# Hybrid decoder trunk: the low parts of the tokens on Pool, and the norm before the experts in two halves

## What is computed

```python
for layer in range(DEPTH):                       # 2
    mix = even_mixer(...) if layer % 2 == 0 else odd_mixer(...)
    x = layer_norm(DN_ALPHA * x + mix, ln1_g[layer], ln1_b[layer])
    ff = moe_ffn(x, router_w[layer], ...)        # top 8 of 64 experts, 4 of 8 groups, and a shared expert
    x = layer_norm(DN_ALPHA * x + ff, ln2_g[layer], ln2_b[layer])
```

## Time and profile before

| | |
|---|---|
| median of 3 runs | 1240.02 us (1238.58 to 1240.29) |
| the profiled execution | 1239.59 us |
| its span | 1237.9 us, 18023 instructions |
| PE busy | 1181.5 us (95%) |
| DVE busy | 401.8 us (32%) |
| ACT busy | 297.8 us (24%) |
| Pool busy | 29.1 us (2%) |
| chain that ended last, by engine | PE 79%, DMA 15%, DVE 4%, ACT 1% |
| data moved by DMA | 445.19 MB, mean 360 GB/s |

### The profile page before, as it was taken

One profiled execution on the slowest core, in us unless ns is written; L12 is line 12 of the kernel. 1 busy time (PEld: TensorE's weight loads), 2 busy tenths in 40 slices (PEclk: granted clock), 3 DMA queues, 4 the chain that ended last, 5 costly groups with the idle time before them and its releaser, 6 DMA issues.

```text
span 1237.9 us, 18023 instructions
## 1 busy us (share of the span) xinstructions
PE 1181.5 (95%) x7212; PEld 539.4 (44%) x7212; DVE 401.8 (32%) x900; ACT 297.8 (24%) x652; POOL 29.1 (2%) x104
## 2 busy tenths in 40 slices
PE   8998999999999999999879999999999999999985
PEld 5776754434333433434236555343443434343421
DVE  3767274212121211212243656322221212121223
ACT  3354332212121211222121353121221112121212
POOL 1005000000000000000000000000000000000000
PEclk9999999999999999999999999999999999999998
DMA  9408059999999999999993657899999999999993
GB/s 368 176 1 315 37 211 424 415 416 426 429 428 429 427 429 427 430 428 428 424 390 139 272 204 279 351 415 411 427 429 428 429 428 429 428 429 429 427 425 146
DMA packets 44177, 445.19 MB, mean 360 GB/s; under 512 B 8016, under 2 KB 9168, under 8 KB 18016
## 3 DMA queue, kind: packets, MB, share of 16 engines
q1 hardware_dynamic: 43824, 444.25, 85.9%
q10 hardware_dynamic: 304, 0.26, 0.1%
HBM read 443.45 MB, written 1.05 MB: 359 GB/s over the span
## 4 chain that ended last, share of the span: by engine, by line
PE 79%; DMA 15%; DVE 4%; ACT 1%; issue 1%; DVEq 0%; SPq 0%
PE psum L429 29%; PE psum L510 16%; DMA w_down_ring<-in_moe_down 10%; PE psum L443 5%; PE psum L517 5%; PE psum L2522 4%; PE psum L2371 4%; PE psum L1392 3%; DMA w_up_ring<-in_moe_up 3%; PE psum L679 2%; PE psum L492 1%; PE psum L1875 1%; PE psum L713 1%; PE psum L2528 1%; PE psum L1703 1%
## 5 line engine op out<-in xcount | busy, mean ns | idle before, releaser
L429 PE MATMUL psum<-w_up_ring,moe_x_selected 128*64 128x512 f32 x2048 | 461.1, 597 | 12.3 <-DMA w_up_ring<-in_moe_up 11.8
L429 PEld LDWEIGHTS psum<-w_up_ring,moe_x_selected 128*64 128x64 f32 x2048 | 139.6, 137 | 296.7 <-issue 277.8
L1219 DVE TENSOR_TENSOR moe_out_low<-psum,moe_out_high 128x512 fp32r<-128x512 f32 x128 | 88.1, 691 | 356.7 <-ACT moe_out_high L968 356.7
L510 PE MATMUL psum<-w_down_ring,moe_hT 128*32 128x512 f32 x1536 | 178.6, 596 | 6.1 <-DMA w_down_ring<-in_moe_down 5.2
L968 ACT CAST moe_out_high<-psum 128x512 fp32r<-128x512 f32 x128 | 74.6, 586 | 262.0 <-PE psum L510 188.1
L1209 DVE SCALAR_TENSOR_TENSOR moe_h<-moe_silu,moe_slot_gate,psum 128x256 f32<-128x256 f32 x64 | 30.7, 480 | 285.6 <-ACT moe_silu L947 285.3
L510 PEld LDWEIGHTS psum<-w_down_ring,moe_hT 128*32 128x32 f32 x1536 | 44.2, 109 | 112.5 <-issue 100.4
L947 ACT ACTIVATE moe_silu<-psum 128x256 f32<-128x256 f32 x64 | 24.5, 383 | 208.1 <-PE psum L429 208.1
L951 ACT COPY moe_hT<-psum 128x256 f32<-128x256 f32 x64 | 23.8, 372 | 199.1 <-PE psum L492 199.1
L517 PE MATMUL psum<-moe_out_high,moe_matchT 128*128 128x512 f32 x128 | 57.0, 445 | 1.5 <-DVE moe_out_low L1219 1.5
L2371 PE MATMUL psum<-w_up_ring,mixed_transposed 128*128 128x512 f32 x128 | 56.6, 594 | 0.7 <-ACT mixed_transposed L2146 0.7
(11 more groups left out here) (537 smaller groups left out, 1012.4 us busy)
## 6 DMA issues: line engine op xcount, KB each, us to landing
w_up_ring<-in_moe_up SPq DMA_DIRECT2D x128, 2048.0 KB, 19.7
w_down_ring<-in_moe_down SPq DMA_DIRECT2D x48, 2048.0 KB, 20.6
norm_and_tokens<-in_moe_down SPq DMA_DIRECT2D x12, 2048.0 KB, 16.8
w_up_ring<-in_ev_columns SPq DMA_DIRECT2D x4, 2048.0 KB, 16.7
w_up_ring<-in_od_w_in SPq DMA_DIRECT2D x4, 2048.0 KB, 18.0
w_up_ring<-in_ev_out SPq DMA_DIRECT2D x2, 2048.0 KB, 8.1
moe_first_down<-in_moe_down SPq DMA_DIRECT2D x2, 2048.0 KB, 10.0
norm_and_tokens<-in_moe_down SPq DMA_DIRECT2D x4, 1024.0 KB, 11.6
```

The source lines that it names most:

```text
L429: last = nc.tensor.matmul(k.psum[e * SLOTS:(e + 1) * SLOTS, bank, :], xsel[:, kk, own:own + SLOTS], up_view(par, e, kk), start=kk == 0, st ...
L510: last = nc.tensor.matmul(k.psum[e * CAPACITY:(e + 1) * CAPACITY, unit_bank[n], :], hT[:, e // 2, own:own + CAPACITY], places[e][:, j, :], ...
L1219: nc.vector.tensor_tensor(low[:, own], k.psum[:, unit_bank[n], :], high[:, own], ALU.subtract).then_inc(s.low, 1)
```

## The change

- `low_part` moves from DVE to Pool, for both tiles. Pool waits there for the normed tile and for the high part. DVE waits for `parts` once, before it adds high and low again at the end.
- The last step of the first norm is two instructions of 512 columns, each with a signal on `normed1`, which now counts to two for each tile. PE waits for one half before four of the eight transposes; ACT's high part, Pool's low part and SP's load wait for both.

```diff
--- before.py
+++ after.py
@@ -561,7 +561,7 @@
             sp.wait_ge(s.mixed, 1 + e)
             load_up_half(sp, k, d, layer, 1, 1, e - 2, gu[1][e - 2])
         sp.dma_start(k.mixT[:].rearrange("p k t -> p (k t)"), d.shared_down[layer]).then_inc(s.shared_wd, 16)
-        sp.wait_ge(s.normed1, NT)
+        sp.wait_ge(s.normed1, 2 * NT)
         load_down_part(sp, norm_down, d, layer, 1, 1, 0, x.dn_norm)
         sp.wait_ge(s.xT_psum, 2 * NT)
         sp.wait_ge(s.parts, NT)
@@ -659,8 +659,8 @@
                 output_product(nc, k, t, half, chunks, begin=False).then_inc(s.mixed, 1)
 
         def turn_x(t):
-            pe.wait_ge(s.normed1, t + 1)
             for b in range(2):
+                pe.wait_ge(s.normed1, 2 * t + b + 1)
                 for c in range(4):
                     last = nc.tensor.transpose(k.psum[:, 4 + b, c * P:(c + 1) * P], k.x[:, t, (4 * b + c) * P:(4 * b + c + 1) * P],
                                                k.ident[:])
@@ -908,7 +908,7 @@
                                k.psum[:, 4 + b, :].rearrange("p (c n) -> p c n", c=4)).then_inc(s.xT, 1)
 
         def high_part(t):
-            act.wait_ge(s.normed1, t + 1)
+            act.wait_ge(s.normed1, 2 * t + 2)
             nc.scalar.copy(x_high[:, t].rearrange("p k c -> p (k c)"), k.x[:, t, :]).then_inc(s.x_high, 1)
 
         def scores(t):
@@ -1053,6 +1053,15 @@
     def gpsimd(pool):
         mixer.gpsimd(pool)
 
+        def low_part(t):
+            pool.wait_ge(s.normed1, 2 * t + 2)
+            pool.wait_ge(s.x_high, t + 1)
+            nc.gpsimd.tensor_tensor(x_low[:, t].rearrange("p k c -> p (k c)"), k.x[:, t, :],
+                                    x_high[:, t].rearrange("p k c -> p (k c)"), ALU.subtract).then_inc(s.parts, 1)
+
+        for t in range(NT):
+            low_part(t)
+
         def gates_of(q):
 
             nc.gpsimd.tensor_copy(quad_gates[:], gate_parts[:, :, bass.ds(8 * q, 8), :]).then_inc(s.quad_gates, 1)
@@ -1075,25 +1084,20 @@
         step(nc.vector.memset(w.ln_eps[:], LN_EPS))
         nc.vector.memset(w1.ln_eps[:], LN_EPS).then_inc(s.eps, 1)
 
-        def low_part(t):
-            dve.wait_ge(s.x_high, t + 1)
-            dve.wait_ge(s.normed1, t + 1)
-            nc.vector.tensor_tensor(x_low[:, t].rearrange("p k c -> p (k c)"), k.x[:, t, :],
-                                    x_high[:, t].rearrange("p k c -> p (k c)"), ALU.subtract).then_inc(s.parts, 1)
-
         for t in range(NT):
             for half in range(2):
                 dve.wait_ge(s.mixed, 2 * t + half + 1)
                 step(residual(nc, k, w1, t, half))
                 step(statistics(nc, dve, step, w1, t, half))
-                if (t, half) == (1, 0):
-                    low_part(0)
             nc.vector.bn_aggr(w1.meanvar[:, t, :], w1.bn[:, t, :, :]).then_inc(s.variance1, 1)
             dve.wait_ge(s.variance1, t + 1)
             step(gain_centred(nc, k, w1, t, w1.meanvar[:, t, 0:1], ALU.subtract))
             dve.wait_ge(s.root1, t + 1)
             step(nc.vector.reciprocal(w1.rstd[:, t:t + 1], w1.root[:, t:t + 1]))
-            scale_shifted(nc, k, w1, t).then_inc(s.normed1, 1)
+            for half in range(2):
+                cols = slice(half * BANK, (half + 1) * BANK)
+                nc.vector.scalar_tensor_tensor(k.x[:, t, cols], w1.resid[:, t, cols], w1.rstd[:, t:t + 1], k.ln[:, 1, cols], ALU.mult,
+                                               ALU.add).then_inc(s.normed1, 1)
 
         def group_heads(t):
             dve.wait_ge(s.scores, t + 1)
@@ -1134,7 +1138,6 @@
         dve.wait_ge(x.router, 32)
         group_heads(0)
         select(0)
-        low_part(1)
         place_of(0)
         first_match(0, s.early_match)
         group_heads(1)
@@ -1267,6 +1270,7 @@
         with dve.Fori(1, QUADS - 1) as q:
             quad(q)
         dve.wait_ge(s.down, 8 * (QUADS - 2) + 6)
+        dve.wait_ge(s.parts, NT)
         for t in range(NT):
             step(nc.vector.tensor_tensor(k.x[:, t, :], x_high[:, t].rearrange("p k c -> p (k c)"),
                                          x_low[:, t].rearrange("p k c -> p (k c)"), ALU.add))
```

## The result

The changed kernel takes **1243.28 us** (median of 20 runs, 1239.71 to 1244.94), the kernel before on the same chip 1240.82 us (20 runs, 1238.48 to 1242.70). The ratio is 1.0018, with an interval of 1.0012 to 1.0024: **2.2 us slower, 1.5 to 3.0**. The forecast was +0.8. What happened is rival two with both races lost: Pool was first at the selection too.

The account below looks back on a forecast made before the run. Weight loads pace the expert loops' ends, but DVE's path to the first match matrix before them carries through one for one. Pool holding the match adds +0.48 and +0.34, +0.8 on 1240.02: 1240.8 us, range 1238.3 to 1242.4.

Parts of the forecast that it names:

- rival two: Selection of tile 0: Pool starts first and holds DVE; +0.98 and +0.85 us, 1241.3 with one race lost, 1241.9 both; chance 0.14.
- who is first at the selection: Selection of tile 0: DVE's L1123 starts before Pool's subtract, by 0.05 us in layer 0 and 0.13 in layer 1.
- Two of 512 columns: First norm on DVE: two halves take about 1.3 us where one instruction takes 1.28; DVE loses 0.02 at most.
- The low part of tile 0: Moved to Pool: no gain in layer 0, where DVE makes it while waiting for PE; about 0.20 us in layer 1.
- Pool starts some 0.06 later: Subtract of tile 1, layer 0: Pool starts 0.06 us after ACT's high part ends at 184.04, so at 184.10.
- Pool's subtract: Low part of 128x1024 on Pool: taken as 2.2 us, bounds 1.85 and 2.9.
- the forecast's own case: Before the experts: DVE's selection passes, the match matrix is held by Pool; +0.48 and +0.34 us; chance 0.60.
- the lock: DVE beside Pool: with two SBUF inputs the later instruction waits; held DVE ends at Pool's end plus its time less 0.13.
- rival one: Match matrix of tile 0: small repeated operands don't hold the port, DVE isn't held; -1.4 us, 1238.6 us; chance 0.20.
- one for one to the end: Between mixer and experts: each microsecond gained or lost there reaches the end of the expert loop in full, in each layer.
- the token load: SP issues its second half about 0.8 us later; hidden by the weight stream, up to 0.8 us were the queue empty.
- the halves on PE: Transposes after the first norm: the earlier half signal wins PE nothing in layer 0, 0.06 us at most in layer 1.

Follow-up runs that it names:

- experiment 1: The changed kernel with the norm put back to one instruction, both low parts still on Pool; 1240.96 us, ratio 1.0001 to the kernel before.
- experiment 4: The changed kernel, with Pool's subtract of tile 1 waiting until DVE has signalled the selection of tile 0; 1243.07 us, ratio 1.0016 to the kernel before.
- experiment 5: The changed kernel with Pool's subtracts replaced by memsets of other tiles and ACT writing zeros as low part; 1239.69 us, ratio 0.9988 to the kernel before.
- experiment 7: Against experiment 1 (low parts on Pool, norm whole): match and add get one operand from PSUM, copied by ACT; 1239.58 us, ratio 0.9983 to the kernel before.
- experiment 10: The kernel before, with the low part of tile 1 made five times on DVE, four to no use; 1252.72 us, ratio 1.0097.
- experiment 9: The kernel before, with SP holding the second half of the token load until both first match matrices are made; 1240.23 us, ratio 0.9998.
- experiment 2: The kernel before, with only the norm in two halves and its signals, both low parts on DVE; 1242.04 us, ratio 1.0011.
- experiment 3: Only the low part of tile 0 on Pool, that of tile 1 on DVE, norm whole; 1241.11 us, ratio 1.0000 to the kernel before.
- experiment 8: The kernel before, low parts on DVE, with slot numbers and router's bias read from PSUM; 1241.02 us, ratio 0.9999.

## Why the prediction was right and wrong

**Wrong: who is first at the selection.** The failed step is the one that put L1123 at 184.04 ahead of Pool at 184.10, with "margins 0.05 and 0.13 us". In the change that instruction (now L1127) was issued 0.07 us behind Pool in layer 0 and 0.08 behind it in layer 1. Three terms under the step were mis-sized: two took from DVE's lead, and one gave. Counted from the product's end in layer 0:

- "Two of 512 columns take about 0.6 + 0.69 = 1.3 us": they take 1.41 where the whole took 1.28. The selection comes 0.13 later.
- The low part of tile 0 was costed at nothing for DVE in layer 0. Without it DVE takes up the last residual at 0.12 in place of 0.04. That moves the norm of tile 1 from 3.25 to 3.33 and the selection with it (7.38 before, 7.46 in experiment 1). ACT's high part doesn't move (it ends at 7.37 before and at 7.38 in experiment 1), so the 0.08 comes off DVE's lead. All seven kernels in which DVE doesn't make this low part show it, after 0.92 to 2.09 us of idle time where DVE was idle for 0.76 before; what makes the difference no run tells apart.
- "Pool starts some 0.06 later" than ACT's end, by PE's pick-up: it takes 0.14 (183.57 to 183.71). That alone works for DVE, by 0.08.

Together 0.06 - 0.13 - 0.08 + 0.08 = -0.07, as measured. In layer 1 DVE came 0.24 later than predicted (7.59 where 767.5 means 7.35), by the same first two terms, and Pool 0.02 later (7.51 for 7.49).

The halves don't delay ACT's high part, since it stands behind ACT's copies of the transposed tile, and PE's transposes start 4.73 after the product before and 4.72 with the change. So ACT, and Pool behind it, kept their time (7.52 with halves, 7.53 without) while DVE lost 0.13, more than its lead. From experiment 1 the lead without the halves is 0.07; with them DVE is behind by 0.07. I had written that a margin of 0.02 was enough at 103.93, and gave the outcome 0.14 although my own margin was half of an error that I would have admitted on any of its terms.

**Mis-sized: Pool's subtract**, 2.35 us where I took 2.2. With 2.35 the forecast's own case would have been +1.1; rival two, which I had at +0.98 and +0.85, measured +1.23 and +1.03 at the marks: 0.15 a layer is the subtract, and 0.08 in layer 0 Pool's later pick-up. My 1241.9 for it also stood on 1240.02, the median of three runs, where the twenty runs beside the change give 1240.82. The line through 64 and 256 columns (2.33) was the nearest. The GPSIMD Engine Reference of the Trainium skill (section 3.1) gives 4497 ns for 2048 columns, an estimate of 2.25 us, 0.1 short.

**Right: the lock.** The held instruction ends at Pool's end plus its own time less 0.13 to 0.15: 186.15 for 186.06, 186.63 for 186.36 in experiment 1, 185.75 for 185.47 in experiment 4. The Trainium skill (SBUF — State Buffer, "Who interferes with whom") adds that "Issue order, not op shape, decides who blocks", and that a GpSimd instruction which only writes does not contend. Experiments 1 and 4 agree with the first (0.07 us turns 0.22 into 2.37), experiment 5 with the second (0.22 inside a memset of 0.53).

**Right: the sign against rival one.** Small repeated operands are held like whole tiles (1.75 for 0.42). Its price is right too: with the hold removed, experiments 5 and 7 show -1.4 and -1.3 where it had -1.4.

**Right: one for one to the end.** Experiment 10 shows it at +11.5 for +12.0. In all kernels the loop of layer 0, from its first expert product to the first transpose of layer 1, lasts 452.7 to 453.9 us, that of layer 1 460.3 to 461.9, whatever came before. Where the stream stood still at 776 in the earlier trace rows, it now stands still from 780 on:

```profile
776.00:778.00 2.00, 1.62 (x7) 1.03 (x8) 1.62 (x8) 0.34 (x1) 0.00 (x0) 1.00 1.00 422
778.00:780.00 2.00, 2.00 (x17) 1.70 (x17) 1.18 (x4) 1.17 (x2) 0.00 (x0) 1.00 0.09 33
780.00:782.00 2.00, 2.00 (x12) 0.72 (x10) 1.77 (x6) 0.00 (x0) 0.00 (x0) 1.00 0.00 0
```

**Right: the token load** (SP's stretch is 5.51 us long in place of 4.70; counted from the product it ends 1.0 later, where 0.8 was foreseen, and experiment 9 shows that this costs nothing) **and the halves on PE** (experiment 2). Of the 0.20 us that leaving DVE should win at 760.38, 0.12 is there: the residual starts 0.11 after the product (762.83) in place of 0.23.

**The division of the loss,** then: relative to before, low parts on Pool with DVE just first +1.3, and the halves, by turning the race, another +1.0. The second is a jump, not a cost: 0.13 us of work made 0.5 us a layer. Without the race it would have cost nothing, since the places wait for PE: the match is issued at 8.41 in experiment 1 and in experiment 5, though the selection ends at 7.68 in the one and at 7.81 in the other, and PE's count (L685) ends at 8.03.

**The spread that is not the edits'.** The stretch from the first transpose of layer 1 to its last product takes 114.7 to 114.8 us in four traces (before, experiments 3, 4 and 5) and 116.5 to 117.3 in the eight others. The granted clock parts them in the same way. At the border of the layers it falls to 0.50 in all twelve; counted from that first transpose it is back at 1.00 after 5.5 to 6.0 us in the four and after 6.9 to 8.7 us in the eight. And in the eight alone it falls once more, between 723 and 735 us. Before:
```profile
722.00:726.00 4.00, 3.71 (x36) 3.08 (x35) 2.16 (x8) 1.97 (x4) 0.00 (x0) 1.00 0.88 335
726.00:730.00 4.00, 3.94 (x41) 2.93 (x38) 3.03 (x6) 3.97 (x15) 0.00 (x0) 1.00 1.09 435
```

and with the change:
```profile
722.00:726.00 4.00, 4.00 (x23) 3.29 (x23) 1.61 (x7) 0.60 (x1) 0.00 (x0) 0.85 0.57 192
726.00:730.00 4.00, 4.00 (x42) 3.45 (x40) 1.15 (x4) 3.35 (x5) 0.00 (x0) 0.72 1.11 431
```

It doesn't go with the edits: experiments 8 and 9, which keep Pool idle as before, are among the eight, and experiments 3, 4 and 5, in which Pool works, among the four. The kernel before alone shows as much: of its executions beside the experiments, the 11 with a mean clock of 0.988 took 1242.1 us on average and the 6 with 0.992 took 1240.1. This may be why the totals of experiments 1, 2 and 7 lie up to 1.2 us beside their two layers, all within or at the edge of their intervals. Why the clock falls the second time, with PE busy all through, stays open.

## What to carry to other kernels

Before moving an elementwise step to Pool, list DVE's instructions with two SBUF inputs that will be issued while it runs, on either side of every close start, and price the hold for each: Pool's end plus the held one's own time. Where one of them is on the path, give it an operand in PSUM, or leave the step on DVE. And where an outcome hangs on a lead smaller than the error of the terms under it, it is a coin toss, and deserves the chance of one.

## What the runs showed of the hardware that was not expected

- A lead of 0.07 us is worth 2.15 us to the instruction that has it (0.22 in experiments 1 and 7 against 2.37 in the change), in both layers.
- One operand in PSUM frees a DVE instruction from Pool wholly (0.42 against 1.75), at no price of its own (experiment 8: ratio 0.9999).
- Pool picks up ACT's signal 0.14 to 0.15 us after ACT's end, and DVE's after 0.18 (182.94 to 183.12, experiment 4).
- Two 512-column instructions with a signal each take 0.13 us longer on DVE than one of 1024 (1.41 for 1.28).
- In layer 0 DVE takes up the last residual 0.04 us after the modelled end of PE's product when the low part of tile 0 came just before, and 0.11 to 0.12 after it when DVE had been idle since the statistics.
- In experiment 10, where the wait for DVE leaves PE idle from 186 to 190 and from 778 to 782, the granted clock falls to 0.50 behind it, and delays of 5.04 and 5.05 us grow to 6.05 and 5.45.
